# Eight dilated heads computed in two softmax parts and joined by their denominators, with the second block's weight units split inside both projections

## The chip, the cores and the metric

The kernel runs on one core of one Trainium2 chip. The metric is the device time in microseconds (us) of one execution, the median of a few runs. The core's engines work side by side and meet at semaphores: PE (TensorE: matrix products and transposes into PSUM), DVE (VectorE), ACT (ScalarE), POOL (GpSimd) and SP, which here does nothing but start transfers. ACT and POOL start transfers as well.

## The reference, cut to what matters

Two transformer blocks over 1024 tokens of width 1024. The first block's attention has 16 heads of width 64, eight dilated and eight of a 16 x 64 grid neighbourhood. A dilated head mixes three patterns:

```python
DIL_PATTERNS = ((128, 1), (512, 4), (2048, 16))
def dilated_mixture_attention(q, k, v, slopes):
    results = [dilated_window_attention(q, k, v, slopes, w, d) for (w, d) in DIL_PATTERNS]
    outs, lses = jnp.stack([r[0] for r in results]), jnp.stack([r[1] for r in results])
    weights = jax.nn.softmax(lses, axis=0)
    return jnp.sum(weights[..., None] * outs, axis=0).astype(q.dtype)
```

A query t sees the keys within 64 tokens, the keys within 256 tokens at a distance that 4 divides, and all keys at a distance that 16 divides, each with a bias of slope times distance. The mixture weighted by the log-sum-exps is one softmax in which a key counts as often as patterns hold it. So the keys of a query are a near band (|d| <= 64) and a far part of the same residue mod 4 (256 of 1024 keys). After attention come an RMS norm of each half of the heads, W_out, a router and 16 experts, and then the second block, whose first projection uses w_in2.

## The kernel before, in words

Every float32 product is made of three: a weight or activation x is split into hi (x rounded by a cast) and lo (x - hi), and hi*hi, hi*lo and lo*hi are summed. POOL splits weights: `split(n)` is a CAST (L661) and a TENSOR_TENSOR (L665) of 128x1024, one pair for each "unit" of weights, and PE has about 10.9 us of products for a unit.

**QKV projection.** 24 units of w_in (16 for Q and K, 8 for V). ACT takes a unit's result out of PSUM (L1412) in the order m = 0..23. Beside it DVE prepares tables for the second block's S5 scan: small operations first (helpers at L1795, L1800), then the first norm's spread root (L1746), which PE must have after unit 6, then eight sets of "turns" (L1929 to L1938). ACT sends a set off (L1418) in between its evacuations: for 6 <= m < 14 it waits for `turns_ready` and then issues the transfer, so a later evacuation stands behind it. PSUM has four slots, so PE can be a few units ahead of ACT.

**Attention.** One loop on each engine over steps t, 128 units: head u // 8, query tile u % 8. For unit u PE makes `scores` (L982: a 128-query tile against all 1024 keys for heads 0 to 7, against 256 or 384 keys for heads 8 to 15), DVE adds the bias and takes the row's maximum (L1984), ACT exponentiates with the sum (L1424), PE transposes (`turn`, L991), ACT copies (L1433), PE multiplies with the values (`mix`, L1005), DVE scales by the reciprocal (L1993, L1995). PE does scores(t), turn(t-2), mix(t-3) in a step. For each head POOL makes the split queries and keys QS, KH, KL, each half of the partitions (L697 to L703: three casts, three subtractions of 64x1024), starts the load of the head's bias strip, and then does `split_in2(h)` (L674, L676): one unit of w_in2. SP stores the two results to DRAM (w2_parts), waits, loads the next raw unit, and fills x_slots (the expert blocks' rows) with zeroes, 31 transfers of 512 KB in pieces of 512 bytes.

**End of attention.** Squares (L1440), a root, eight scalings of the dilated half at step T_SCALE (ACT copies turned blocks at L1453, the "f" copies) and of the other half at the end (DVE L2005), turned by `turn_na` (L1016) inside the first W_out units. SP gets to the loads of w_out (L633) after the last w_in2 unit is stored. The first two W_out units run together (`first_pair`, L865): k = 0..3 are the dilated half, k = 4..7 need the other half, with their lo parts (DVE L2010).

Of the kernel before, what the change touches and what calls it, by code (L numbers as in the profile page):

```python
# [18 lines left out]
STRIP = 1920  # L19
# [8 lines left out]
KSPLIT = 6  # L28
FF = 22
# [29 lines left out]
def key_tiles(h, i):  # L59

    if h < 8:
        return 0, 8
    return max(i - 1, 0), min(i + 2, 8)


def build(nc, xT, params, w_in, w_out, w_moe, w_in2, w_out2, w_up, w_down, dil_strip, na_strip, s5_b, s5_c, out):
# [5 lines left out]
    w2_parts = nc.dram_tensor("w2_parts", (18, 2, P, S), f32, kind="Internal").ap()  # L72
    s5_turns = nc.dram_tensor("s5_turns", (8, P, 2, S), f32, kind="Internal").ap()

    ctx = ExitStack()
    with ctx:
# [32 lines left out]
        negm = sb("negm", [P, 4])  # L109
        den = sb("den", [P, 8])  # L110
# [18 lines left out]
        def by_rows(ap):  # L129

            return ap.rearrange("p (c r) -> p r c", r=NA_ROWS)

        def by_columns(ap):

            return ap.rearrange("p (r c) -> p c r", c=NA_COLS)

        def columns(ap):

            return ap.rearrange("p (c r) -> p c r", r=NA_ROWS)

        def mat(name, c=0, n=P):
# [10 lines left out]
        x_again = sem("x_again")  # L152
# [4 lines left out]
        zero_set, slots_zeroed, x_scattered = sem("zero_set"), sem("slots_zeroed"), sem("x_scattered")  # L157
# [7 lines left out]
        member_ready, rank_read, dispatch_ready, xtm_ready = (  # L165
            sem("member_ready"), sem("rank_read"), sem("dispatch_ready"), sem("xtm_ready"))
# [4 lines left out]
        gains_ready, tsq_ready, tsum_taken, tvar_ready, troot_ready, tdiag_ready, hn_ready, hres_ready = (  # L171
            sem("gains_ready"), sem("tsq_ready"), sem("tsum_taken"), sem("tvar_ready"), sem("troot_ready"),
# [3 lines left out]
            sem("sq_ready"), sem("sq_added"), sem("sums_ready"), sem("std_ready"))  # L176
        parked, vt2_ready, low_split = sem("parked"), sem("vt2_ready"), sem("low_split")
# [7 lines left out]
        up_scaled, slots_ready = sem("up_scaled"), sem("slots_ready")  # L185
        qk_scaled, cst_again = sem("qk_scaled"), sem("cst_again")
# [5 lines left out]
        gdiff_ready, gexp_done, tdiff_ready, texp_done = (  # L192
            sem("gdiff_ready"), sem("gexp_done"), sem("tdiff_ready"), sem("texp_done"))
# [4 lines left out]
        conv_ready, gates_ready, tanh_ready, root_ready, ggate_ready, rg_ready = (  # L198
            sem("conv_ready"), sem("gates_ready"), sem("tanh_ready"), sem("root_ready"), sem("ggate_ready"), sem("rg_ready"))
        s5b_ready, s5bT_ready, s5x_ready, s5y_ready, s5g_ready, s5s_ready, s5_ready = (  # L200
            sem("s5b_ready"), sem("s5bT_ready"), sem("s5x_ready"), sem("s5y_ready"), sem("s5g_ready"), sem("s5s_ready"), sem("s5_ready"))
# [5 lines left out]
        conv0_ready, conv1_ready, gelu_ready, ffact_ready = (  # L207
            sem("conv0_ready"), sem("conv1_ready"), sem("gelu_ready"), sem("ffact_ready"))
# [17 lines left out]
        parts_order = list(range(0, U_OUT)) + list(range(U_IN2, U_OUT2)) + list(range(U_OUT, U_IN2)) + list(range(U_OUT2, len(units)))  # L226
# [13 lines left out]
        loads, raw_loads = {}, {}  # L240
        into = [0] * RING
        for u in parts_order:
            at_ring = 0 if in2(u) else ring_at(u)
            into[at_ring] += 16
            (raw_loads if in2(u) else loads)[u] = into[at_ring]
# [306 lines left out]
        troots = small[:, 6:8, :]  # L552


        @block.sync
        def _(sp):
            def experts():

# [2088 lines left out]
```

## Time and profile before

| | |
|---|---|
| time, median of 3 runs | 2444.22 us (2443.25 to 2449.57) |
| the profiled execution's own time, span | 2445.05 us, 2443.2 us |
| mean granted clock of PE | 0.964 |
| PE busy | 2263.9 us (93%) |
| PE weight load, DVE, POOL, ACT busy | 1774.0, 1165.3, 985.5, 578.2 us |

The span is what the profiler saw of one execution; its own time is the device time of the same execution. Busy times of engines overlap and don't add. With PE busy for 93% of the span, the kernel's time is nearly the time of PE's work where PE has work, and the question is where it hasn't.

### The profile page before, as it was taken

Reading aid. Unit: us, or ns where it says so; the run is one execution under the profiler, and the core shown is the slowest. Engines: PE = TensorE matmul, PEld = TensorE weight load, DVE = VectorE, ACT = ScalarE, POOL = GpSimd, SP = SyncE. Lnnn points to the kernel's source line nnn. Section 1 sums busy time; section 2 is a strip of 40 time slices with the busy share of each in tenths; the row PEclk is TensorE's granted clock in tenths of the full one; section 3 lists DMA queues with packets and bytes.
Section 4 is the critical chain, followed back from the end, with each engine's and each line's share of the span. In section 5 each row is a group of like instructions: output and inputs, shape, how many; then the busy total and the mean of one; then the engine's idle time right before and its main releaser. Section 6 shows DMA issues by size and latency. Waiting matters only on the chain.

```text
span 2443.2 us, 28063 instructions
## 1 busy us (share of the span) xinstructions
PE 2263.9 (93%) x10832; PEld 1774.0 (73%) x10832; DVE 1165.3 (48%) x1895; ACT 578.2 (24%) x831; POOL 985.5 (40%) x600
## 2 busy tenths in 40 slices
PE   7999999997699499999599998899999999999997
PEld 5888799987576366665376556678788888888875
DVE  7996644446413222222588777755432233143145
ACT  3101255566533111111231005221210011011011
POOL 2333554468623765700303862233323333333324
PEclk9999999998899699999799999899999999999998
DMA  4231154335622787822722221211111111111103
GB/s 156 78 121 70 42 188 144 120 110 170 201 99 113 271 301 299 324 104 97 280 76 86 103 74 47 104 38 49 43 46 50 52 48 39 61 50 39 58 26 112
DMA packets 89392, 274.33 MB, mean 112 GB/s; under 512 B 6896, under 2 KB 38768, under 8 KB 82096
## 3 DMA queue, kind: packets, MB, share of 16 engines
q1 hardware_dynamic: 71120, 188.84, 22.1%
q0 software_dynamic: 8064, 42.80, 4.8%
q10 hardware_dynamic: 10080, 40.90, 4.3%
q8 instruction: 90, 1.47, 0.2%
q14 instruction: 38, 0.31, 0.0%
HBM read 195.97 MB, written 76.55 MB: 112 GB/s over the span
## 4 chain that ended last, share of the span: by engine, by line
PE 79%; DVE 8%; POOL 5%; DMA 4%; issue 3%; ACT 2%; SPq 0%; DVEq 0%; POOLq 0%; ACTq 0%
PE ps L883 15%; PE ps L885 15%; PE ps L887 15%; PE ps L1005 5%; PE ps L1102 4%; PE ps L982 3%; PE ps L991 3%; PE ps L1086 2%; PE ps L1082 2%; PE ps L1084 2%; PE ps L1083 2%; PE ps L865 1%; PE ps L868 1%; PE ps L867 1%; PE ps L1070 1%
## 5 line engine op out<-in xcount | busy, mean ns | idle before, releaser
L883 PE MATMUL ps<-work_part 128*128 128x512 f32 x1760 | 547.9, 393 | 2.6 <-DVE work L2385 1.7
L887 PE MATMUL ps<-work_part 128*128 128x512 f32 x1760 | 542.4, 389 | 0.0
L661 POOL CAST work_part<-ring 128x1024 fp32r<-128x1024 f32 (+2 forms) x124 | 118.5, 956 | 786.1 <-PE ps L887 659.6
L883 PEld LDWEIGHTS ps<-work_part 128*128 128x128 f32 x1760 | 329.8, 188 | 76.9 <-issue 6.5
L887 PEld LDWEIGHTS ps<-work_part 128*128 128x128 f32 x1760 | 330.6, 188 | 69.2
L885 PE MATMUL ps<-work_part 128*128 128x512 f32 x1152 | 354.6, 389 | 0.0
L665 POOL TENSOR_TENSOR work_part<-ring,work_part 128x1024 fp32r<-128x1024 f32 (+2 forms) x124 | 281.2, 2268 | 15.9 <-PE ps L1300 6.1
L885 PEld LDWEIGHTS ps<-work_part 128*128 128x128 f32 x1152 | 216.2, 188 | 44.9
L885 PE MATMUL ps<-hT_part,work_part 128*128 128x512 f32 x608 | 188.0, 390 | 0.0
L1005 PE MATMUL ps<-work,hT 128*128 128x64 f32 x1376 | 174.3, 276 | 2.6 <-ACT hT L1433 2.1
L2033 DVE TENSOR_TENSOR hT<-ps,hT 128x1024 f32<-128x1024 f32 x40 | 49.0, 1225 | 261.5 <-PE ps L887 245.0
L1005 PEld LDWEIGHTS ps<-work,hT 128*128 128x128 f32 x1376 | 167.5, 195 | 6.8 <-ACT hT L1433 3.8
L885 PEld LDWEIGHTS ps<-hT_part,work_part 128*128 128x128 f32 x608 | 114.4, 188 | 24.1
L1984 DVE CUSTOM_DVE_ANT_0 hT<-ps,hT 128x1024 f32<-128x1024 f32 (+2 forms) x86 | 75.1, 874 | 116.0 <-PE ps L982 113.0
L982 PE MATMUL ps<-work_part 128*128 128x512 f32 (+2 forms) x384 | 115.3, 410 | 15.5 <-issue 7.9
L1701 ACT ACTIVATE work<-ps,cst 128x1024 f32<-128x1024 f32 x22 | 26.6, 1208 | 398.2 <-DVE ps L2455 398.2
L739 POOL TENSOR_TENSOR experts_lo<-pages,experts_hi 128x1024 fp32r<-128x1024 f32 x48 | 113.5, 2365 | 11.1 <-DMA pages<-w_moe 7.7
L1102 PE MATMUL ps<-pages,work 128*128 x248 | 111.6, 592 | 1.6 <-DVE work L2165 1.6
L865 PE MATMUL ps<-work_part 128*128 128x512 f32 x160 | 66.3, 414 | 48.3 <-POOL work_part L665 18.8
L1424 ACT ACTIVATE hT<-hT,negm 128x1024 f32<-128x1024 f32 (+2 forms) x86 | 74.6, 868 | 92.9 <-DVE negm L1984 92.7
L2455 DVE TENSOR_TENSOR ps<-ps,cst 128x1024 f32<-128x1024 f32 x22 | 27.1, 1232 | 144.2 <-PE ps L887 137.6
L1433 ACT ACTIVATE hT<-ps 128x1024 f32<-128x1024 f32 (+2 forms) x128 | 92.8, 725 | 0.8 <-PE ps L991 0.7
(376 smaller groups left out, 3490.2 us busy)
## 6 DMA issues: line engine op xcount, KB each, us to landing
pages<-w_moe SPq DMA_DIRECT2D x16, 2048.0 KB, 9.7
ring<-w_up_units SPq DMA_DIRECT2D x44, 512.0 KB, 3.2
ring<-w_in_units SPq DMA_DIRECT2D x42, 512.0 KB, 3.7
w_parts<-work_part SPq DMA_DIRECT2D x36, 512.0 KB, 3.6
work_part<-w_parts SPq DMA_DIRECT2D x36, 512.0 KB, 4.1
pages<-w_moe SPq DMA_DIRECT2D x16, 1024.0 KB, 7.0
x_slots<-hT SPq DMA_DIRECT2D x31, 512.0 KB, 5.2
work<-x_slots ACTq DMA_DIRECT2D x31, 512.0 KB, 5.7
```

The lines of the kernel that those rows point to most:

```text
L661: pool.tensor_copy(WHI[n % 2][:, 0:cols], w).then_inc(whi_ready, 1)
L665: pool.tensor_tensor(WLO[n % 2][:, 0:cols], w, WHI_F[n % 2][:, 0:cols], ALU.subtract).then_inc(wlo_ready, 1)
L739: lo = pool.tensor_tensor(XLOW[:, at_lo:at_lo + S], w, hi.bitcast(f32), ALU.subtract)
L865: mm = pe.matmul(pss[i][:, c], ws[i][0][:, w], hi[k][:, c], start=(k == 0), stop=(lo is None and k == last))
L883: pe.matmul(ps[:, c], whi[:, w], hi[k][:, c], start=(k == 0), stop=False)
L885: pe.matmul(ps[:, c], whi[:, w], lo[k][:, c], start=False, stop=False)
L887: mm = pe.matmul(ps[:, c], wlo[:, w], hi[k][:, c], start=False, stop=(k == len(hi) - 1))
L982: mm = pe.matmul(ps[:, b * HALF:b * HALF + w], QS[h % 2][:, i * P:(i + 1) * P], part[h % 2][:, c0:c0 + w], start=(part is KH), stop=(part ...
L1005: mm = pe.matmul(ps[:, 0:DH], PT[u % 2][:, j * P:(j + 1) * P], Wp[16 + k0 + j][:, h * DH:(h + 1) * DH], start=(j == 0), stop=(j == k1 - k0 ...
L1102: mm = pe.matmul(ps[:, half * HALF:(half + 1) * HALF], HAT[b % 2][:, f * P:(f + 1) * P], xw[:, bass.ds(pages[b] + 4 * S + f * S + half * H ...
L1433: act.activation(PT[u % 2][:, 0:(k1 - k0) * P], PS[bank(n)][:, 0:(k1 - k0) * P], ACT.Copy).then_inc(pT_ready, 1)
L1984: dve.tensor_tensor_reduce(out=banks(SB[u % 3][:, 0:nk]), in0=scores, in1=banks(bias), scale=-1.0, scalar=3.0e38, op0=ALU.add, op1=ALU.min ...
```

## The change

A dilated head becomes four units instead of eight (`NU` = 64 instead of 128). Units q = 0, 1 are the far part: four groups of 128 queries of one residue mod 4, each against that residue's 256 keys; units q = 2, 3 are the near band: four query tiles each against 256 keys around the tile. Each unit has four segments of 256 columns, with a maximum and a sum of its own. K and V of the dilated heads are stored by residue. The far part's output, maximum and sum (66 numbers a query) go through DRAM (`turn_rows`) to come back in token order, and `merge_diffs` (DVE), `merge_exps` (ACT), `merge_weights` (DVE) and `merge` (POOL) join them with the near part. Neighbourhood heads get four units of two tiles each. The other halves of KH and KL are copied by transfers (`double`, SP) instead of two POOL operations. The w_in2 units are split by POOL after units 1 to 12 of the QKV projection (`EARLY`) and after units 26 to 31 in W_out (`LATE`), from buffers of their own; the zeroing of x_slots moves to ACT's queue during V's units. The steps `T_SQ, T_ROOT, T_SCALE, T_TURN, T_PART` move with the shorter loop. Several semaphores are merged with no other effect on the order.

```diff
-STRIP = 1920
+STRIP = 896
+EARLY, LATE = 12, 6
+NR, NA_ = 4, 256
+HEAD_ROW = DH + 2
...
-        NU = NH * NT
-        T_SQ, T_ROOT, T_SCALE, T_TURN, T_PART = 72, 82, 84, 86, 97
+        T_DIFF, T_EXP, T_WEIGHT = 10, 11, 12
+        T_SQ, T_ROOT, T_SCALE, T_TURN, T_PART = 44, 48, 49, 51, 60
...
+            def double(h):
+
+                own, other = halves_of(h)
+                sp.wait_ge(qk_parts, 4 * (h + 1))
+                for part in (KH, KL):
+                    sp.dma_start(part[h % 2][other, :].bitcast(f32), part[h % 2][own, :].bitcast(f32)).then_inc(dup_loaded[h % 2], 16)
+
+            def turn_rows(h):
+
+                sp.wait_ge(heads_done, 4 * h + 2)
+                sp.dma_start(head_rows[h % 2].rearrange("(u p r) e -> p r u e", u=2, r=NR), OB[h % 2].rearrange("p (r u) e -> p r u e", u=2)).then_inc(rows_stored, 16)
+                sp.wait_ge(rows_stored, 16 * (h + 1))
+                if h >= 2:
+                    sp.wait_ge(merged, h - 1)
+                sp.dma_start(OBN[h % 2], head_rows[h % 2].rearrange("(t p) e -> p t e", p=P)).then_inc(rows_loaded[h % 2], 16)
...
-                    sp.wait_ge(zero_set, 1)
-                    for n in range(U_OUT2 - U_IN2):
-                        park_in2(n)
-                        for b in range(2 * n, min(2 * n + 2, NBLK)):
-                            if b >= 4:
-                                sp.wait_ge(scores_ready, NU // (NBLK + 1) * (b - 3))
...
+                    double(0)
+                    load_near_values()
+                    double(1)
+                    for h in range(2, NH):
+                        if h < 10:
+                            turn_rows(h - 2)
+                        double(h)
...
+            def merge(h):
+
+                far, rows = OBN[h % 2][:, :, 0:DH], bT[:, :, h * DH:(h + 1) * DH]
+                w = [stats(h, 2 + n).unsqueeze(2).to_broadcast([P, NT, DH]) for n in range(2)]
+                pool.wait_ge(weights_ready, h + 1)
+                pool.wait_ge(heads_done, 4 * h + 4)
+                pool.tensor_tensor(far, far, w[1], ALU.mult)
+                link(pool.tensor_tensor(rows, rows, w[0], ALU.mult))
+                pool.tensor_tensor(rows, rows, far, ALU.add).then_inc(merged, 1)
+                pool.wait_ge(merged, h + 1)
 
             for n in range(24):
                 split(n)
+                if 1 <= n <= EARLY:
+                    split_in2(n - 1)
...
-                pool.tensor_tensor(KL[h % 2][other, :], k[own, :], KH[h % 2][own, :].bitcast(f32), ALU.subtract).then_inc(qk_parts, 1)
-                pool.tensor_copy(KH[h % 2][other, :], k[own, :]).then_inc(qk_parts, 1)
...
-                pool.wait_ge(qk_parts, 6 * h + 6)
-                split_in2(h)
...
+                if 3 <= h < 11:
+                    merge(h - 3)
...
             for n in range(26, 32):
                 split(n)
+                split_in2(EARLY + n - 26)
...
+                if t % 4 == T_DIFF % 4 and 0 <= t - T_DIFF < DIL_UNITS:
+                    merge_diffs((t - T_DIFF) // 4)
+                if t % 4 == T_WEIGHT % 4 and 0 <= t - T_WEIGHT < DIL_UNITS:
+                    merge_weights((t - T_WEIGHT) // 4)
```

POOL in the QKV projection of the changed kernel, from the split of unit 4 on (part_loaded is the arrival of a raw w_in2 unit):

```order
L773 CAST work_part<-ring 128x1024 [waits mm_done,w_loaded0,wlo_ready]
L777 TENSOR_TENSOR work_part<-ring,work_part 128x1024 [waits whi_ready]
L783 CAST work_part<-work 128x1024 [waits part_loaded1]
L785 TENSOR_TENSOR work_part<-work,work_part 128x1024 [waits whi_ready]
L773 CAST work_part<-ring 128x1024 [waits mm_done,w_loaded1,wlo_ready]
```

Before, the rows at L773 and L777 (there L661 and L665) followed one another with nothing between; now a pair of w_in2 stands between every two of units 1 to 13.

POOL in attention, one dilated head of the kernel before:

```order
L697 CAST work_part<-work 64x1024 [waits qk_parts,wlo_ready]
L698 CAST work_part<-work 64x1024
L700 TENSOR_TENSOR work_part<-work,work_part 64x1024 [waits qk_parts]
L701 TENSOR_TENSOR work_part<-work,work_part 64x1024
L702 TENSOR_TENSOR work_part<-work,work_part 64x1024
L703 CAST work_part<-work 64x1024
L712 DMA hT<-dil_strip 128x1920
L674 CAST work_part<-ring 128x1024 [waits parked,w_loaded0,qk_parts]
L676 TENSOR_TENSOR work_part<-ring,work_part 128x1024 [waits whi_ready]
```

and of the changed one (head 0's merge, then head 4's splits and strip):

```order
L801 TENSOR_TENSOR hT<-hT 128x8x64 [waits heads_done,weights_ready]
L802 TENSOR_TENSOR work<-work,hT 128x8x64
L803 TENSOR_TENSOR work<-work,hT 128x8x64 [waits pool_link]
L826 CAST work_part<-work 64x1024 [waits qk_parts,mm_done,qk_scaled,merged]
L827 CAST work_part<-work 64x1024
L829 TENSOR_TENSOR work_part<-work,work_part 64x1024 [waits qk_parts]
L830 TENSOR_TENSOR work_part<-work,work_part 64x1024
L835 DMA hT<-dil_strip 128x896 [waits scores_ready]
```

The merge of head h-3, which waits for DVE's weights, now stands ahead of the splits of head h+1.

SP in attention of the changed kernel (the copies of head 3's keys, the row transfers of head 2, the copies of head 4's keys):

```order
L669 DMA work_part<-work_part 64x1024 [waits qk_parts]
L669 DMA work_part<-work_part 64x1024
L674 DMA head_rows<-hT 512x2x66 [waits heads_done]
L678 DMA hT<-head_rows 128x8x66 [waits merged,rows_stored]
L669 DMA work_part<-work_part 64x1024 [waits qk_parts]
L669 DMA work_part<-work_part 64x1024
```

Where stores of w_in2 units and zeroes stood, the copies for a head's keys now stand behind the row transfers of the head two earlier, and behind the wait for the first of them to land.

## Rows read from the trace of the kernel before

**Rows 1.** Windows: stretch, us, busy of each engine, PEclk, DMA share, GB/s.

```profile
85.30:205.30 120.00, 120.00 (x528) 98.67 (x527) 113.82 (x338) 14.79 (x10) 39.07 (x22) 1.00 0.30 110
294.30:522.00 227.70, 224.96 (x1739) 209.88 (x1740) 103.33 (x253) 137.22 (x192) 120.73 (x78) 1.00 0.43 143
522.00:651.10 129.10, 112.52 (x743) 100.07 (x742) 74.76 (x273) 83.86 (x228) 101.00 (x63) 0.92 0.53 172
```

**Rows 2.** Timeline, DVE and POOL around one split: start, duration, engine, line.

```profile
75.08 0.17 DVE L1795 TENSOR_SCALAR small<-small 128x2 f32<-128x2 f32 x1
...
75.29 1.06 POOL L661 CAST work_part<-ring 128x1024 fp32r<-128x1024 f32 x1 [7.35 <-PE ps L887]
75.48 0.90 DVE L1795 TENSOR_SCALAR small<-small 128x2 f32<-128x2 f32 x1
...
76.44 2.41 POOL L665 TENSOR_TENSOR work_part<-ring,work_part 128x1024 fp32r<-128x1024 f32 x1
76.61 2.26 DVE L1795 TENSOR_SCALAR small<-small 128x2 f32<-128x2 f32 x1
```

**Rows 3.** Timeline, DVE and ACT in the QKV projection.

```profile
85.53 1.23 DVE L1746 TENSOR_TENSOR work<-std,cst 128x1024 f32<-128x1024 f32 x1
...
96.95 1.97 ACT L1412 ACTIVATE work<-ps 128x1024 f32<-128x1024 f32 x1 [8.89 <-PE ps L887]
...
205.67 0.33 ACTq L1418 DMA_DIRECT2D s_turns<-work  x1
...
219.36 1.03 ACT L1412 ACTIVATE work<-ps 128x1024 f32<-128x1024 f32 x1 [9.58 <-PE ps L968]
```

**Rows 4.** Timeline, one step of a dilated head.

```profile
380.29 1.19 PE L982 MATMUL ps<-work_part 128*128 128x512 f32 x4
...
381.52 1.23 DVE L1984 CUSTOM_DVE_ANT_0 hT<-ps,hT 128x1024 f32<-128x1024 f32 x1 [1.88 <-PE ps L982]
...
383.90 0.48 PE L982 MATMUL ps<-work_part 128*128 128x512 f32 x1
```

**Rows 5.** Timeline, POOL's parts of a head.

```profile
590.34 2.36 POOL L700 TENSOR_TENSOR work_part<-work,work_part 64x1024 fp32r<-64x1024 f32 x1
```

**Rows 6.** Groups by line, busy, mean ns: a copy of 1024 columns.

```profile
L2172 DVE COPY work<-ps 128x1024 f32<-128x1024 f32 x5 | 6.1, 1224 | 12.8 <-PE ps L1102 12.8
```

**Rows 7.** DMA issues: KB each, median us from issue to landing.

```profile
x_slots<-hT SPq DMA_DIRECT2D x31, 512.0 KB, 5.2
...
outT<-hT SPq DMA_DIRECT2D x16, 256.0 KB, 2.2
```

**Rows 8.** Timeline, steps of a neighbourhood head.

```profile
635.78 0.42 DVE L1984 CUSTOM_DVE_ANT_0 hT<-ps,hT 128x256 f32<-128x256 f32 x1 [1.36 <-DMA hT<-na_strip]
...
636.25 0.51 ACT L1424 ACTIVATE hT<-hT,negm 128x256 f32<-128x256 f32 x1 [1.21 <-DVE negm L1984]
...
638.33 0.62 PE L982 MATMUL ps<-work_part 128*128 128x384 f32 x2
...
640.00 0.45 PE L982 MATMUL ps<-work_part 128*128 128x384 f32 x1 [0.34 <-DVE work L1995]
```

**Rows 9.** Timeline, steps in which dilated tiles are turned and copied.

```profile
576.02 0.59 PE L982 MATMUL ps<-work_part 128*128 128x384 f32 x2 [1.15 <-issue]
...
578.91 0.59 PE L982 MATMUL ps<-work_part 128*128 128x384 f32 x2 [1.15 <-issue]
```

**Rows 10.** Timeline, from the end of attention into W_out.

```profile
658.51 3.25 DVE L2005 TENSOR_SCALAR work<-work,small 128x512 f32<-128x512 f32 x8
...
662.30 11.12 SPq L633 DMA_DIRECT2D ring<-w_out_units  x6
...
669.89 0.77 PE L865 MATMUL ps<-work_part 128*128 128x512 f32 x1 [18.79 <-POOL work_part L665]
...
681.97 1.92 PE L1016 MATMUL ps<-cst,work 128*128 128x128 f32 x16
...
689.39 0.50 PE L865 MATMUL ps<-work_part 128*128 128x512 f32 x1 [2.77 <-DVE work_part L2010]
```

More of the change, by code:

```diff
@@ L225, in build @@
         split_of = {u: n for n, u in enumerate(split_units)}
-        parts_order = list(range(0, U_OUT)) + list(range(U_IN2, U_OUT2)) + list(range(U_OUT, U_IN2)) + list(range(U_OUT2, len(units)))
+        parts_order = []
+        for u in range(0, U_IN2):
+            parts_order.append(u)
+            if 1 <= u <= EARLY:
+                parts_order.append(U_IN2 + u - 1)
+            if u >= U_IN2 - LATE:
+                parts_order.append(U_IN2 + EARLY + u - (U_IN2 - LATE))
+        parts_order += list(range(U_OUT2, len(units)))
         order_of = {u: n for n, u in enumerate(parts_order)}
@@ L238, in wparts @@
             return WHI[split_of[u] % 2], WLO[split_of[u] % 2]
-        loads, raw_loads = {}, {}
+        loads = {}
         into = [0] * RING
         for u in parts_order:
-            at_ring = 0 if in2(u) else ring_at(u)
-            into[at_ring] += 16
-            (raw_loads if in2(u) else loads)[u] = into[at_ring]
+            if in2(u):
+                continue
+            into[ring_at(u)] += 16
+            loads[u] = into[ring_at(u)]
             if u == U_IN2 - 1:
@@ L315, in build @@
         U_QKV += [take(1) for m in range(2, 7)]
-        n_mix = add_late_norm(Hp, "norm_mix", [Wp[22], Wp[23], Wp[15]], mix_use, take(1), (BHI, [hTr[t][:, :] for t in range(NT)]))
+        n_mix = add_late_norm(Hp, "norm_mix", [Wp[22], Wp[23], Wp[11]], mix_use, take(1), (BHI, [hTr[t][:, :] for t in range(NT)]))
         U_QKV += [take(1) for m in range(7, 16)]
@@ L633, in _ @@
                     sp.dma_start(ring[:, ring_at(u), 0:src.shape[-1]], src).then_inc(w_loaded[ring_at(u)], 16)
+                if u == 4:
+                    load_in2(0)
+                    load_in2(1)
+                if 5 <= u < EARLY + 5:
+                    park_in2(u - 5)
+                if u == U_OUT + 5:
+                    sp.wait_ge(mm_done, done(use_o[NU - 1]))
+                    load_in2(EARLY)
+                    load_in2(EARLY + 1)
+                if u == U_IN2 - 1:
+                    for n in range(EARLY, EARLY + LATE):
+                        park_in2(n)
             for half in range(2):
@@ L711, in _ @@
[L711 to L719 removed]
+                    pool.wait_ge(scores_ready, PARTS_DONE[4 * (h - 1)])
@@ L1397, in _ @@
             for m in range(24):
-                if m >= 16:
-                    if m == 16:
-                        for i in range(4):
-                            act.wait_ge(turns_stored[i], 32)
+                if m == 16:
+                    for i in range(4):
+                        act.wait_ge(turns_stored[i], 32)
+                    link(act.activation(ZERO, ident, ACT.Copy, scale=0.0))
+                if m == 23:
+                    act.wait_ge(slots_zeroed, 16 * NBLK)
+                if m in (12, 14):
+                    act.wait_ge(parked, 32 * (EARLY - 1 + (m - 12) // 2))
                 n = U_QKV[m] if m < 16 else U_V[m - 16]
@@ L1432, in copy_pT @@
                     act.wait_ge(mm_done, done(use_o[u - 2]))
-                act.activation(PT[u % 2][:, 0:(k1 - k0) * P], PS[bank(n)][:, 0:(k1 - k0) * P], ACT.Copy).then_inc(pT_ready, 1)
+                act.activation(PT[u % 2][:, cols], PS[bank(n)][:, cols], ACT.Copy).then_inc(pT_ready, 1)
             def heads_square(half, i):
-                act.wait_ge(heads_done, (7 + 8 * half) * NT + i + 1)
+                if half == 0:
+                    act.wait_ge(merged, 8)
+                else:
+                    act.wait_ge(heads_done, NU - 4 + i // 2 + 1)
                 if half + i:
```

460 lines of the change are left out of this document (283 added, 177 removed).

## The prediction

> **What bounds the kernel now.** I read the windows by stage first. In the QKV projection PE is busy for all of 120.00 us of the stretch 85.3 to 205.3, but DVE has 113.82 of the same 120: one engine is the bound and another has nearly no room. In the dilated heads' stretch PE is busy for 224.96 of 227.70, in the neighbourhood heads' for 112.52 of 129.10 [rows 1]. So PE's work sets the dilated heads, and links between engines take 16.6 us from the neighbourhood heads. Then the timeline from the end of attention: the stretch ends at 651.1, W_out starts at 669.89 after a wait for POOL's split, which had waited for a load that SP issued only at 662.30 [rows 10].
>
> **The change, part by part.**
>
> *QKV projection, +32.* POOL's pair for one unit is a CAST of 1.06 and a TENSOR_TENSOR of 2.41, with 120.00 us for 528 products, 48 to a unit, or 10.9 us a unit of PE's work over it [rows 1, 2]; twelve more pairs fit in POOL's time. They don't fit in DVE's. A DVE operation that takes 0.17 us took 0.90 beside the CAST and 2.26 beside the TENSOR_TENSOR: DVE stood until POOL's instruction was over, 0.73 + 2.09 = 2.8 us for one split [rows 2]. This is what a port held by one of the two looks like. The Trainium skill, "SBUF — State Buffer", § Who interferes with whom, has the rule for it (the shared port pair is an exclusive lock, the engine that comes first keeps it for its instruction); the trace agrees at 0.90 and 2.26, and by the rule the delay is a whole instruction for each split, as the rows have it. Twelve added splits cost DVE 12 x 2.8 = 34, and the longer DVE works the more ordinary splits it meets, one each 10.9 us: 3 to 4 more in the 34 us, of which I take 2, 5.6 (the late sets need not meet each). That is 40. DVE's last set of turns, sent off at 205.67, comes at about 245.7. What slack is there? ACT takes the first V unit transposed at 219.36, 9.6 us after it was free for it, and DVE was ready before [rows 3]. The same 10 us lie at the front: the norm's root is done at 85.53 + 1.23 = 86.8 and unit 6, which it must follow, at 96.95 [rows 3]. So 40 - 10 = 30 reach PE. I expect about 17 of it at the norm's root after unit 6, and 13 at the evacuations behind `turns_ready`. A PE that has stood so long restarts at the lower clock (after the idle before 669.89 a product took 0.77, the one at 689.39 took 0.50 [rows 10]): 2 more.
>
> *Dilated heads.* Before, a step takes 383.90 - 380.29 = 3.6 us of PE [rows 4], eight to a head. A unit after is as many PE columns: scores of 8 products of 256 against 4 of 512, the same 8 turns, 8 groups of two in place of a chain of eight in the mix. So a unit costs PE 3.65 and a head 14.6 instead of 29: the work halves because half the units are gone. But a new chain goes round through the engines. The scores of head h+1 wait for `double(h+1)`, that waits for POOL's splits of h+1, and those stand behind merge(h-3) in POOL's order. The merge waits for DVE's `merge_weights(h-3)`, which DVE does in step 4h, behind the bias and maximum of head h's first scores. So a head's splits can't begin before the head ahead of it has begun. Its length, from rows: from the first scores on, DVE's bias of 1024 columns 1.23 [rows 4], now in four pieces, 1.5; the evacuating copy of 256 columns a quarter of 1.22 [rows 6] plus its fixed part, 0.4; five small operations with a link each at 0.2, 1.0; PE's scores before it 1.2 [rows 4]; sum 4.1. POOL's three merges of 512 columns, half of 2.36 each [rows 5], plus three links, 3.8; sum 7.9. The splits, two casts of 1.05 and two subtractions of 2.36, 6.9; sum 14.8. The pair of 256-KB copies: issue 0.33 twice [rows 3] and a landing of 2.2 by the 256-KB row [rows 7], or 2.9; sum 17.7 to 18.4. I take 18.2 a head, against PE's 14.6. Nothing in it runs beside anything else of it. Heads 3 to 7: 5 x 18.2 = 91. Head 0 needs nothing of POOL in attention but its own splits: 10.4 from the stretch's start, which lies a unit into it. Heads 1 and 2 have no merge ahead, but their copies behind the row transfers: 16 each, 32.
>
> ACT has four exponentials of 256 columns at 0.51 [rows 8] and a copy of 1.03 (the 1024 columns at 219.36 [rows 3]) in a unit, 3.05 of 3.65: not the bound.
>
> *Neighbourhood heads.* POOL still does the merges of heads 5 to 7 ahead of the splits of heads 9 to 11 (3 x 17.3 = 52 for heads 8 to 10; the first scores are shorter). The last 20 steps: a tile took 640.00 - 638.33 = 1.67 with 0.34 of it idle [rows 8], so two tiles in a unit are 2.7 of PE and one link where two were, 2.75. Twelve steps less one, 11 x 2.75 = 30.3. In the eight steps with f copies ACT's queue puts copy_f between copy_pT and the next exponentials: before a step took 578.91 - 576.02 = 2.9 [rows 9], and with two tiles' worth in ACT it is 2.9 + 0.9 (a wider exponential and copy) + 0.4 (a second bias) = 4.2: 33.6. Squares and table loads 3, the tail of three steps without scores 6. Together 72.9.
>
> Attention after: 10.4 + 32 + 91 + 52 + 72.9 = 258.3, before 227.7 + 129.1 = 356.8 [rows 1]: -98.5.
>
> *W_out's start, -15.2.* Call the end of attention E (651.1, where the last window of [rows 1] ends). Before, k = 4 of the first pair starts at 689.39, E + 38.3 [rows 10]. Now the w_in2 stores are not ahead of the w_out loads on SP, and POOL's split(24) runs as soon as the last scores are done, so PE's k = 0..3 start before the other half's scales. Those end for four tiles at 658.51 + 4 x 0.4 = E + 9 [rows 10]; the first turns stand there, four groups of six products, 6 x 120.00/528 = 1.36 each [rows 1], lie between, and the second turns start at E + 15.7. From there to k = 4 it was 689.39 - 681.97 = 7.4 [rows 10], so E + 23.1.
>
> *At nothing.* The LATE pairs in W_out: POOL has two pairs of 3.5 [rows 2] a unit against 10.9 of PE; their cover gone, 6 x 3.5 = 21 at the most, and DVE's work there is little. The zeroing, 31 transfers that were on SP beside attention, is now 31 x 512 KB beside V's units; its price is hidden unless SP's weight loads come late (a range term, 0 to 8). DVE's merge weights, the smaller strips and merged semaphores lie in other engines' gaps.
>
> Sum: 2445.05 + 32 - 98.5 - 15.2 = 2363.4; the profiled execution was 0.8 over the median, so 2362.
>
> **The rivals.**
>
> *(a) The round through POOL is hidden* (the chain is shorter than 14.6, or queued early enough). Then heads 1 to 7 cost 14.6 and heads 8 to 10 about 11, a gain of 7 x 3 + 3 x 6.5 = 40: 2322. For it: POOL was busy for only 120.73 of 227.70 [rows 1]. Against: the order of its rows, merge ahead of splits.
>
> *(b) DVE's delay doesn't reach PE* (the added splits fall where DVE has its PSUM or one-operand work). 2362 - 32 = 2330. Against: 113.82 busy of 120 [rows 1], whatever the operation.
>
> *(c) The row transfers are slow.* The far rows are 1024 pieces of 264 bytes out and in, and `double(h+2)` stands behind the landing of head h's store. The store starts in step 4h+5 and head h+2 needs its keys in step 4h+8, so a second way round is the store's time S, the copies' 2.9, a step of 3.65 and a link or two: S + 7.5. It is longer than 18.2 from S = 10.7 on. The nearest row, 1024 pieces of 512 bytes, has 5.2 with neighbours in flight [rows 7]: hidden. If S is 15 to 18, eight heads (2 to 9) take 22.5 to 25.5 in place of 18.2: 34 to 58 more, 2396 to 2420. The Trainium skill, "DMA: Bandwidth & Descriptors", § Specifications, speaks for it: below 512 bytes the engines read, modify and write. No row here shows a smaller piece; by it the store might take twice the zeroing's time, 10.4, an estimate, which is still hidden.
>
> *(d) Slower than before.* Only (c) carried further does it. My sum has 82 us to lose over eight heads, 10.2 each: a period of 28.4, an S of 21, four times the zeroing's 5.2 [rows 7]. At S = 23 the time is 2461.
>
> **How the numbers follow.** My own course 0.64, (a) 0.12, (b) 0.10, (c) 0.10, (d) 0.02, and 0.02 for what none of them holds. The bounds of unknown prices: the delay of QKV from 0 to 45, the chain 14.6 to 20 a head (-40 to +16), the W_out start from -10 to -20, the hidden parts up to +8. The range 2314 to 2408 holds my course, (a), (b) and the near half of (c). Within 0.3% (7 us, about what a measurement tells from no change) is hardly a case: it needs (c) with S just at 21. Faster (my course, (a), (b), (c)) 0.96, same 0.01, slower 0.03, with half of the unnamed rest.
>
> **What would show it.** In the changed kernel's trace: PE idle for some 17 us after unit 6, with DVE's L1746 row late at about 114 against 85.5; the first V evacuation near 250 against 219. In attention, heads' first scores released by the copies of keys (L669), 18 us apart, and POOL's cast released by `merged`. At W_out, k = 4 at 23 us after the last mix. The prediction is wrong if POOL's splits are ready a head ahead, if DVE's small operations don't stand beside the new pairs, or if a row store lasts over 10.

## The result, and the profile after

The changed kernel takes 2421.68 us (median of 4 runs, 2419.63 to 2423.71) against 2445.59 for the kernel before on the same chip: a ratio of 0.9901, interval 0.9883 to 0.9918. That is 24 us less. I had forecast 2362, 82 less, with a range of 2314 to 2408: the direction is right, the size is wrong by more than the range allows. Later runs of the kernel before, beside the experiments, had medians of 2442.6, 2442.8 and 2442.0, so a difference of medians between an experiment and the changed kernel comes out up to 4 us larger than by the ratios.

Where did it go? I read the times at which the stages meet. First ACT's row in the V units and PE's in attention:

```profile
247.45 1.03 ACT L1567 ACTIVATE work<-ps 128x1024 f32<-128x1024 f32 x1
...
316.25 1.03 ACT L1567 ACTIVATE work<-ps 128x1024 f32<-128x1024 f32 x1 [10.78 <-PE ps L1082]
329.42 1.02 ACT L1567 ACTIVATE work<-ps 128x1024 f32<-128x1024 f32 x1 [12.14 <-DMA x_slots<-work]
```

The first V unit is taken at 247.45, where 219.36 stood [rows 3] and I had expected about 250. The last but one is taken at 316.25; in the kernel before the same row stands at 290.10. The last one should follow 3 us later, as it did before (293.20), and comes at 329.42: what ended its wait is the landing of the zeroes. PE's first scores start at 330.49 instead of 294.3.

The windows of the changed kernel from there (columns as in [rows 1]), head by head for heads 0 to 10, then the last heads, and W_out up to k = 4:

```profile
330.50:342.50 12.00, 10.51 (x68) 10.30 (x69) 5.81 (x32) 10.38 (x35) 4.24 (x3) 0.78 0.41 98
342.50:362.10 19.60, 17.34 (x135) 17.23 (x134) 7.21 (x36) 12.60 (x37) 7.59 (x7) 0.93 0.32 79
362.10:381.80 19.70, 17.76 (x132) 17.62 (x133) 7.54 (x39) 12.04 (x37) 2.63 (x2) 0.91 0.32 79
381.80:405.30 23.50, 18.16 (x133) 18.08 (x133) 9.98 (x44) 12.04 (x37) 10.50 (x8) 0.88 0.29 66
405.30:428.20 22.90, 18.31 (x132) 18.17 (x133) 9.86 (x44) 12.04 (x37) 10.51 (x8) 0.87 0.28 67
428.20:452.40 24.20, 24.17 (x132) 24.20 (x133) 8.24 (x44) 10.88 (x35) 10.45 (x8) 0.60 0.28 64
452.40:474.30 21.90, 16.93 (x135) 16.83 (x134) 10.85 (x44) 13.20 (x41) 10.54 (x8) 0.94 0.29 70
474.30:498.30 24.00, 17.99 (x133) 17.88 (x133) 10.13 (x44) 12.04 (x37) 10.51 (x8) 0.86 0.32 65
498.30:519.70 21.40, 14.09 (x102) 13.81 (x102) 8.97 (x28) 8.27 (x21) 10.51 (x8) 0.82 0.33 72
519.70:541.20 21.50, 11.66 (x82) 11.29 (x82) 8.53 (x32) 7.68 (x21) 10.47 (x8) 0.74 0.21 47
541.20:562.20 21.00, 14.39 (x82) 13.99 (x82) 6.08 (x29) 7.57 (x20) 16.69 (x12) 0.74 0.20 48
562.20:640.00 77.80, 66.51 (x487) 63.80 (x487) 42.96 (x140) 56.27 (x138) 30.40 (x21) 0.92 0.31 85
640.00:664.40 24.40, 17.45 (x81) 14.57 (x80) 5.08 (x12) 15.85 (x21) 1.52 (x2) 0.86 0.58 237
```

Heads 3 to 7 take 22 to 24 us each, not 18.2, and in four of the five PE is busy for 17 to 18 of it. The head from 428.2 on shows a second thing: PE is busy for all of 24.17 us, with the same work, at a granted clock of 0.60. Attention as a whole lasts 640.0 - 330.5 = 309.5 us against 356.8 before. From its end to k = 4 of the first pair it is 24.4, where it was 38.3 [rows 10].

| stretch | forecast | measured |
|---|---|---|
| start of attention | +32 | +36.2 (26.2 at the V unit before the last, 10.0 more at the last) |
| attention | -98.5 | -47.3 |
| its end to k = 4 | -15.2 | -13.9 |
| the rest | 0 | -0.4 |

Sum -25.4, which is what the spans differ by (2443.2 and 2417.8). So nothing behind W_out moves, and one term is wrong by 51.

What does a head wait for? The waits of PE in attention (us in total, times, longest), and the timeline of one round, on PE, POOL and SP:

```profile
PE ps L1095 <- DMA work_part<-work_part: 48.9, 9, 9.9
```

```profile
405.26 2.22 PE L1095 MATMUL ps<-work_part 128*128 128x256 f32 x8 [5.31 <-DMA work_part<-work_part]
...
410.42 1.03 POOL L801 TENSOR_TENSOR hT<-hT 128x512 f32<-128x512 f32 x1 [12.64 <-DVE hT L2184]
...
412.54 1.19 POOL L803 TENSOR_TENSOR work<-work,hT 128x512 f32<-128x512 f32 x1
413.79 1.04 POOL L826 CAST work_part<-work 64x1024 fp32r<-64x1024 f32 x1
...
418.33 2.37 POOL L830 TENSOR_TENSOR work_part<-work,work_part 64x1024 fp32r<-64x1024 f32 x1
...
420.73 1.10 SPq L669 DMA_DIRECT2D work_part<-work_part  x2
...
428.23 2.23 PE L1095 MATMUL ps<-work_part 128*128 128x256 f32 x8 [4.62 <-DMA work_part<-work_part]
```

The round is the one of the forecast, link for link: from the first scores to the merge 5.2 us (forecast 4.1), merge 3.4 (3.8), splits 6.9 (6.9), and from the issue of the two key copies to the scores that wait for them 7.5 (2.9 to 3.6). The copies and row transfers in the table of DMA issues (KB each, median us to landing):

```profile
work_part<-work_part SPq DMA_DIRECT2D x32, 256.0 KB, 6.0
head_rows<-hT SPq DMA_DIRECT2D x8, 264.0 KB, 4.9
hT<-head_rows SPq DMA_DIRECT2D x8, 264.0 KB, 3.1
```

A key copy, 64 partitions of SBUF to 64 others, lands after 6.0 us, where I had taken 2.2 from a transfer of the same size, but from 128 partitions to DRAM [rows 7]. The row transfers in pieces of 264 bytes, which I had feared, land in 4.9 and 3.1.

### The profile page after: what moved, and what is told of

Read it like the earlier page. It is cut to its first block, busy times and chain, and to the rows that moved or that the text cites. A ratio compares the mean times of both kernels' runs of the same rounds, so it can differ in the third digit from the quotient of the medians.

```text
span 2417.8 us, 26338 instructions
## 1 busy us (share of the span) xinstructions
PE 2177.0 (90%) x10096; PEld 1707.9 (71%) x10096; DVE 1163.9 (48%) x1927; ACT 524.3 (22%) x904; POOL 955.9 (40%) x591
## 4 chain that ended last, share of the span: by engine, by line
PE 65%; DVE 17%; DMA 5%; POOL 5%; issue 4%; ACT 4%; SPq 0%; DVEq 0%; POOLq 0%; ACTq 0%
PE ps L997 13%; PE ps L999 13%; PE ps L1001 13%; PE ps L1251 4%; PE ps L1235 2%; PE ps L1231 2%; DMA work_part<-work_part 2%; PE ps L1233 2%; PE ps L1095 2%; PE ps L1232 2%; DVE work L2104 1%; DVE work L2106 1%; PE ps L1155 1%; DVE small L1970 1%; DVE work L2108 1%
## 5 line engine op out<-in xcount | busy, mean ns | idle before, releaser
L773 POOL CAST work_part<-ring 128x1024 fp32r<-128x1024 f32 (+2 forms) x124 | 118.9, 959 | 761.4 <-PE ps L1001 631.3
L997 PEld LDWEIGHTS ps<-work_part 128*128 128x128 f32 x1760 | 330.2, 188 | 79.3 <-issue 6.9
L1001 PEld LDWEIGHTS ps<-work_part 128*128 128x128 f32 x1760 | 330.7, 188 | 69.1
L777 POOL TENSOR_TENSOR work_part<-ring,work_part 128x1024 fp32r<-128x1024 f32 (+2 forms) x124 | 282.3, 2277 | 15.9 <-PE ps L1449 6.1
L999 PEld LDWEIGHTS ps<-work_part 128*128 128x128 f32 x1152 | 216.2, 188 | 44.9
L1095 PE MATMUL ps<-work_part 128*128 128x256 f32 (+2 forms) x416 | 90.2, 364 | 67.6 <-DMA work_part<-work_part 48.9
L999 PEld LDWEIGHTS ps<-hT_part,work_part 128*128 128x128 f32 x608 | 114.7, 189 | 24.2
L1095 PEld LDWEIGHTS ps<-work_part 128*128 128x128 f32 x416 | 75.1, 246 | 70.0 <-issue 58.3
L1155 PE MATMUL ps<-work,hT 128*128 128x64 f32 x864 | 113.8, 288 | 5.2 <-ACT hT L1597 5.2
L1155 PEld LDWEIGHTS ps<-work,hT 128*128 128x128 f32 x864 | 112.6, 209 | 6.4 <-ACT hT L1597 3.6
L2149 DVE CUSTOM_DVE_ANT_0 hT<-ps,hT 128x256 f32<-128x256 f32 (+1 forms) x130 | 52.4, 453 | 118.6 <-PE ps L1095 105.5
L1251 PEld LDWEIGHTS ps<-pages,work 128*128 128x128 f32 x248 | 47.1, 190 | 60.7 <-issue 60.7
```

The lines of the kernel that those rows point to most:

```text
L773: pool.tensor_copy(WHI[n % 2][:, 0:cols], w).then_inc(whi_ready, 1)
L777: pool.tensor_tensor(WLO[n % 2][:, 0:cols], w, WHI_F[n % 2][:, 0:cols], ALU.subtract).then_inc(wlo_ready, 1)
L997: pe.matmul(ps[:, c], whi[:, w], hi[k][:, c], start=(k == 0), stop=False)
L999: pe.matmul(ps[:, c], whi[:, w], lo[k][:, c], start=False, stop=False)
L1001: mm = pe.matmul(ps[:, c], wlo[:, w], hi[k][:, c], start=False, stop=(k == len(hi) - 1))
L1095: mm = pe.matmul(o, lhs, of_part(part), start=(part is keys[0]), stop=(part is keys[1]))
```

## The experiments

**Splits ahead of the merge.** Is the round what costs, or is PE slow by itself? Two orders are exchanged at once, on POOL (splits and merge) and on SP (key copies and row transfers).

```diff
-                if 3 <= h < 11:
-                    merge(h - 3)
+                if 4 <= h < 12:
+                    pool.wait_ge(qk_parts, 4 * h + 4)
+                    merge(h - 4)
...
+                        double(h)
                         if h < 10:
                             turn_rows(h - 2)
-                        double(h)
```

> POOL does the splits of head h before the merge of head h-4 (the merges one head later), and SP starts the key copies of a head ahead of the row transfers. Nothing is left out. Theory (the round of weights, merge, splits and key copies sets a head's time in attention: 21.0 to 24.2 us a head for heads 3 to 10): the splits and copies are ready before PE needs them, a dilated head takes about 15.5 and heads 8 to 10 about 11, so 5 x 7.8 + 3 x 10.3 + some 8 for heads 1 and 2 = about 78 us less than the changed kernel, near 2344. First rival (PE itself is slow in the new units, at the lower clock, whatever it waits for): a head stays above 20 and the time above 2400. Second rival (the row transfers set the head's time): no change either, since they are as before.

2356.18 us (2353.5 to 2361.01), ratio 0.9643, interval 0.9627 to 0.9659: 65 less than the changed kernel, of the 78 expected. In its waits of PE over attention the key copies have all but gone:

```profile
PE ps L1096 <- ACT work L1568: 11.2, 1, 11.2
...
PE ps L1096 <- DMA work_part<-work_part: 1.0, 1, 1.0
```

The window of one dilated head, and its four scores on PE's timeline:

```profile
381.88:398.59 16.71, 16.71 (x134) 16.71 (x134) 8.65 (x44) 12.06 (x39) 10.49 (x9) 1.00 0.46 92
```

```profile
381.88 2.12 PE L1096 MATMUL ps<-work_part 128*128 128x256 f32 x8
...
386.42 2.12 PE L1096 MATMUL ps<-work_part 128*128 128x256 f32 x8
...
390.96 1.41 PE L1096 MATMUL ps<-work_part 128*128 128x128 f32 x10
...
394.79 1.36 PE L1096 MATMUL ps<-work_part 128*128 128x256 f32 x10
```

The head is now all PE, at the full clock. It also shows a second mis-sizing: a far unit takes 4.54 us and a near one 3.83, so a head is 16.7 of PE, not 14.6. Which of the two exchanges gave how much wasn't tried apart. In the changed kernel's round above, SP issues the copies at 420.73, as POOL's last split ends (418.33 + 2.37): for heads 3 to 10 POOL's order counted, and SP's can have counted only for the first heads, whose copies stood behind a row store of 4.7 and 5.0 us.

The whole of attention, from the first scores to W_out's first product, in the changed kernel and in this one:

```profile
330.49:640.53 310.04, 247.86 (x1744) 243.23 (x1745) 136.46 (x557) 175.57 (x494) 135.58 (x98) 0.85 0.30 72
332.00:578.53 246.53, 231.63 (x1744) 228.00 (x1745) 130.64 (x557) 175.40 (x494) 135.74 (x98) 0.94 0.38 90
```

Of the 63.5 us less, 48 are PE's waits for the copies (48.9 down to 1.0). Nearly all the rest, 16.2, is PE's busy time: the same 1744 products at a granted clock of 0.94 instead of 0.85.

**POOL makes the second halves.** Undoes `double` alone (two transfers of 256 KB less, a subtraction and a cast of POOL more in each head).

```diff
-                pe.wait_ge(qk_parts, 4 * (h + 1))
-                pe.wait_ge(dup_loaded[h % 2], 32 * (h // 2 + 1))
+                pe.wait_ge(qk_parts, 6 * (h + 1))
...
+                pool.tensor_tensor(KL[h % 2][other, :], k[own, :], KH[h % 2][own, :].bitcast(f32), ALU.subtract).then_inc(qk_parts, 1)
+                pool.tensor_copy(KH[h % 2][other, :], k[own, :]).then_inc(qk_parts, 1)
```

> Undoes one part of the change: POOL makes the second halves of KL and KH itself (a subtraction and a cast of 64x1024, 3.4 us a head) and the two transfers of 256 KB are gone. Nothing is left out. Theory (the copies' 7.5 us from issue to the first scores is on the path): the round goes from 23.0 to about 19, some 4 less for each of heads 3 to 10 and 3 for heads 1 and 2: about 2385. Rival (the copies are not what is waited for; POOL is): POOL's 3.4 more for each of eight heads comes on top, about 2449.

2398.27 us (2394.22 to 2399.46), ratio 0.9816, interval 0.98 to 0.9833: 21 to 23 less, where 36 was expected and the rival said 27 more. The expected round was 19 us. One is 19.8 (the first merge rows of two heads stand at 404.79 and 424.61), but the seven from 383.70 to 528.05 have a mean of 20.6, against 22.6 in the changed kernel (386.99 to 545.00). One of them is set by PE at the lower clock and not by the round:

```profile
440.50:465.00 24.50, 24.50 (x136) 24.50 (x136) 8.74 (x44) 13.13 (x41) 13.76 (x10) 0.65 0.18 48
```

So the copies were on the path and cost more than the 3.4 us of POOL that they replaced, but by 2 us a round, where I had expected 4.

**Half of each key copy.** From head 2 on a copy moves 512 of 1024 columns.

```diff
+                w = slice(0, S if h < 2 else HALF)
                 for part in (KH, KL):
-                    sp.dma_start(part[h % 2][other, :].bitcast(f32), part[h % 2][own, :].bitcast(f32)).then_inc(dup_loaded[h % 2], 16)
+                    sp.dma_start(part[h % 2][other, w].bitcast(f32), part[h % 2][own, w].bitcast(f32)).then_inc(dup_loaded[h % 2], 16)
```

> On the changed kernel. From head 2 on each key copy moves 512 of the 1024 columns (the rest of the other half keeps older data, so the output is not the reference's); same number of transfers and rows, half the bytes. Theory (the copies' time goes by their bytes, 64 partitions to 64 partitions): a landing of 3.5 to 4 instead of 6, and 2 to 2.5 us less on each of heads 2 to 10, so about 20 less, 2402. Rival (a fixed time to land, or waiting behind other transfers): landing still near 6 and 2417 to 2424.

2401.51 us (2399.93 to 2403.23), ratio 0.9826, interval 0.9805 to 0.9848: the 20 expected. But the landing went only from 6.0 us to 4.7 (median of the 28 halved copies), and PE's wait for the copies from 48.9 to 32.3. Half the bytes took off a fifth of the time: the time expected came, the price by bytes alone did not. What the fixed part is, stays open.

**The early w_in2 splits, narrowed.** Ten of the twelve units have 8 of 1024 columns split.

```diff
+                w = slice(0, 8 if 2 <= n < EARLY else S)
-                pool.tensor_copy(RAW_HI[at], RAW[at]).then_inc(whi_ready, 1)
+                pool.tensor_copy(RAW_HI[at][:, w], RAW[at][:, w]).then_inc(whi_ready, 1)
```

(the subtraction in the same way, and the store of lo takes the tile of hi).

> Leaves out work: ten of the twelve w_in2 units that POOL splits in the QKV projection get only 8 of their 1024 columns split (the stores and loads of these units stay), so the output is not the reference's. Theory (DVE stands while POOL's instruction runs, and that delay reaches PE): DVE's last set of turns is ready some 28 us earlier and the first V unit is taken about 22 to 26 us earlier; 2396 to 2400 in all. Rival (DVE and ACT are late for another reason, the stores and raw loads or the order on ACT's queue): within 5 us of the changed kernel, 2417 to 2424.

2395.02 us (2389.78 to 2396.01), ratio 0.9807, interval 0.9791 to 0.9823: 23 to 27 less. The two last V units are taken at 291.06 and 304.91, 25.2 and 24.5 earlier than in the changed kernel. All transfers were still there, and only ten of POOL's twelve added pairs had become short, so it is these instructions that make DVE late, and with it PE.

**The zeroing divided.** Sixteen blocks in the V units, fifteen copied DRAM to DRAM in attention.

```diff
-                    act.wait_ge(slots_zeroed, 16 * NBLK)
+                    act.wait_ge(slots_zeroed, 16 * ZF)
...
+                        for b in ((ZF, ZF + 1) if h == 2 else (ZF + h - 1,)):
+                            sp.dma_start(x_slots[b * P:(b + 1) * P, :], x_slots[(b - ZF) * P:(b - ZF + 1) * P, :]).then_inc(slots_zeroed, 16)
```

> Of the 31 zeroing transfers 16 stay in the V units on ACT's queue, four a unit; the other 15 blocks are copied from zeroed ones, DRAM to DRAM, by SP in attention, one or two a head. Nothing is left out. Theory (the last V unit's evacuation waits 10 us for the zeroes to land): the last V unit is taken at about 320 instead of 329.4, and the time is about 10 less, 2411. Rival (something else is late there, the values' rows or the first keys' copies, or the copies in attention hold up the key copies): 0 to 10 more, 2421 to 2431.

2413.57 us (2410.62 to 2422.03), ratio 0.9878, interval 0.9861 to 0.9894, which overlaps the changed kernel's: by time alone it is not clear. The trace is:

```profile
319.41 1.03 ACT L1572 ACTIVATE work<-ps 128x1024 f32<-128x1024 f32 x1 [10.76 <-PE ps L1087]
322.59 1.02 ACT L1572 ACTIVATE work<-ps 128x1024 f32<-128x1024 f32 x1 [2.16 <-PE ps L1087]
```

The last V unit follows the one before it by 3.2 us again, released by PE. It is taken 6.8 earlier than 329.42. The one before it is 3.2 later than in the changed kernel; I have no cause for this, but it is at 316.2 to 318.4 in the four other kernels that leave the projection as it is. The profiled execution is the slowest of the four (2422.03; the others 2410.62 to 2413.64), so only this stretch is read from it.

**Both edits.** Splits first, and the zeroing divided.

> Splits ahead of the merge and the zeroing divided, in one kernel, nothing left out. If the two gains are apart in the program (the attention loop, 65 us; the last V unit's wait, 8 us), they add: about 2348. If the fifteen DRAM copies now disturb an attention loop that has become tight (the key copies and row transfers share the queues with them), part is lost: 2352 to 2360.

2348.7 us (2346.05 to 2352.96), ratio 0.9614, interval 0.9591 to 0.9637: 73 less than the changed kernel, where the two alone had 65 and 8: they add, as far as can be told when the runs of one kernel lie 7 us apart.

**Far queries side by side.** On the kernel with the splits first.

```diff
-                        lhs = queries.rearrange("p (u x r) -> p r u x", u=2, r=NR)[:, r, n % 2, :]
+                        lhs = queries[:, n * P:(n + 1) * P]
```

> On the kernel with the splits first. The far units read their queries as 128 neighbouring columns instead of every fourth one, so the scores are of the wrong queries and the output is not the reference's; all counts and sizes are the same. Theory (PE's load of a weight tile with a stride takes 0.24 us instead of 0.12, which shows as 2.12 us for the 8 products of a far unit against 1.36 for 10 of a near one): about 0.75 less for each of 16 far units, 12 in all, 2344. Rival (the far scores are slow for another reason, the keys' columns or the PSUM banks): no change, 2356.

2344.91 us (2336.9 to 2347.7), ratio 0.9582, interval 0.9554 to 0.9609, against 0.9643: 11 to 15 less. In attention's groups of instructions (by form) the scores of 256 columns, first with every fourth column, then with plain queries:

```profile
L1096 PE MATMUL ps<-work_part 128*128 128x256 f32 x256 | 56.7, 359 | 14.6 <-ACT work L1568 11.2 <-issue 2.4 <-DMA work_part<-work_part 1.0
L1096 PE MATMUL ps<-work_part 128*128 128x256 f32 x256 | 43.8, 307 | 15.3 <-ACT work L1568 11.8 <-issue 2.3 <-DMA work_part<-work_part 1.1
```

The 256 products, half of them in far units, take 43.8 us instead of 56.7. The scores of a head's two far units there:

```profile
392.65 1.20 PE L1096 MATMUL ps<-work_part 128*128 128x256 f32 x8
396.27 1.20 PE L1096 MATMUL ps<-work_part 128*128 128x256 f32 x8
```

A far unit is 3.62 us long here instead of 4.54. So the strided weight tile is what makes the far units 0.9 longer, at the full clock. At the lower of PE's two levels it shows much less: in the first heads, at a granted clock of 0.50, eight plain products took 2.05 us (345.96) and eight strided ones 2.21 in the kernel with the splits first (344.34).

**The w_in2 units in the heads.** On both edits, the twelve early units are split in attention again, behind the merge, one a head.

```diff
-                if 1 <= n <= EARLY:
-                    split_in2(n - 1)
...
+                if h in AT_HEAD:
+                    pool.wait_ge(qk_parts, 4 * h + 4)
+                    split_in2(AT_HEAD[h])
```

> On the kernel of both edits: the twelve w_in2 units that were split in the QKV projection are split in attention again, one a head in heads 0 to 7 and 12 to 15, behind the merge; SP stores and loads them there. Nothing is left out. Theory (twelve added pairs cost the projection about 26 us through DVE, and POOL has 5.6 us left of a dilated head's 16.7 with the splits first): the first V unit is back near 219 to 222 and the time about 26 less than the kernel of both edits, 2322. Rival (the attention loop has no room left: POOL's 3.5 more, and the stores' bytes beside the key copies, make PE wait again): the gain in the projection is given back in attention, 2335 to 2350.

2355.71 us (2351.21 to 2357.16), ratio 0.9631, interval 0.9608 to 0.9654: 7 more than without it by the medians, with intervals that overlap, and 34 more than expected. The projection gave back what was expected (the last V unit at 294.04), and attention took 279.6 us (295.1 to 574.7). As the rival said, the gain in the projection was lost in attention, and 6 us more than its 2350. But was it POOL's time? Its DMA issues:

```profile
ring<-w_in_units SPq DMA_DIRECT2D x36, 512.0 KB, 5.9
...
head_rows<-hT SPq DMA_DIRECT2D x8, 264.0 KB, 8.4
```

and POOL's timeline, with an idle time of 4 to 9.5 us ahead of each of the eleven splits from head 1 on, in six of them ended by the raw unit's landing:

```profile
353.77 1.03 POOL L804 CAST work_part<-ring 128x1024 fp32r<-128x1024 f32 x1 [8.49 <-DMA ring<-w_in_units]
```

The row stores land in 8.4 us, where they took 4.9 in the changed kernel and 5.5 in the one with both edits, and POOL stands where it should work. That speaks for the transfers, not POOL's 3.5 us; the next run tries it.

**The zeroes in the projection.** On the last kernel, all zeroing moved to where the DMA queues have room, and the next raw unit loaded as soon as the stores have landed.

```diff
-        ZERO = Wp[23][:, S - P:S]
+        ZERO = Wp[15][:, S - P:S]
...
+                for b in range(3 * (u - 5), min(3 * (u - 4), NBLK)) if u >= 5 else ():
+                    sp.dma_start(x_slots[b * P:(b + 1) * P, :].rearrange("p (k n) -> p k n", n=P),
+                                 ZERO.unsqueeze(1).to_broadcast([P, NT, P])).then_inc(slots_zeroed, 16)
```

> On the kernel with the w_in2 units in the heads. All 31 zeroing transfers now lie in the QKV projection (three after each weight load of units 5 to 15, on SP, from a zeroed part of a tile that K's last unit fills later), the DRAM copies in attention are gone, and the next raw w_in2 unit is loaded as soon as the stores have landed. Nothing is left out. Theory (in the kernel before this one the transfers in attention lay in each other's way: row stores landed in 8.4 us instead of 4.9 and POOL waited 4 to 9 us a head for raw units): row stores land in 5 to 6 again, most of the 34 us lost in attention come back, 2322 to 2335. Rival (POOL's 3.5 us a head itself is too much for the loop, whatever the transfers do): 2345 to 2356.

2328.02 us (2324.36 to 2332.28), ratio 0.9519, interval 0.9493 to 0.9545. This kernel beats both: 114 less than the kernel before, 94 less than the changed one. Its DMA issues and two of its rows:

```profile
ring<-w_in_units SPq DMA_DIRECT2D x36, 512.0 KB, 4.0
...
head_rows<-hT SPq DMA_DIRECT2D x8, 264.0 KB, 6.3
```

```profile
294.23 3.20 PE L1121 MATMUL ps<-work_part 128*128 128x256 f32 x12 [1.11 <-ACT work L1592]
...
552.34 0.47 PE L1005 MATMUL ps<-work_part 128*128 128x512 f32 x1 [0.50 <-DVE work L2184]
```

Attention starts at 294.2, where it started before the change, and W_out at 552.3: 258.1 us with the twelve splits in it, against 279.6 in the last kernel and 248.5 (321.5 to 570.0) in the kernel of both edits, which has none there. So of the 31 us that the splits cost attention at first, 21.5 lay with the transfers. Where are the other 9.6? Windows of 16.7 us, counted from the first scores, show it: the second and the fifth of this kernel, then the second of the kernel of both edits.

```profile
310.93:327.63 16.70, 15.39 (x70) 15.42 (x71) 3.61 (x18) 5.97 (x18) 12.74 (x10) 0.51 0.58 170
361.03:377.73 16.70, 16.70 (x135) 16.70 (x133) 8.67 (x45) 12.05 (x38) 13.91 (x11) 1.00 0.71 193
```

```profile
338.19:354.89 16.70, 16.70 (x120) 16.70 (x121) 6.45 (x34) 9.53 (x30) 0.94 (x1) 0.86 0.31 79
```

In this kernel PE waits 4.56 us for head 1's key copies (2.78 in the kernel of both edits), and then works at 0.51 of the clock through the second window: 70 products instead of 120. The first three windows have 256 products against 323, half a head's work. From the fourth to the eighth PE is busy throughout at 1.00 in both kernels, and a round stays at 16.7 us with the 3.5 us of POOL in it (first merge rows at 375.35 and 392.05). So in those heads POOL's time costs nothing, and most of the 9.6 is lost in the first two. Whether a transfer or POOL's order makes head 1's copies late there wasn't tried. Two things were moved at once here (the zeroes, and the order of the raw load); which of them gave more wasn't tried either.

## Why the prediction was wrong

**The QKV projection: right in mechanism, and nearly in size.** The norm's spread root was late: DVE did it at 114.41, forecast about 114, and PE waited 17.2 us after unit 6, where I had said about 17:

```profile
115.69 3.78 PE L1060 MATMUL ps<-work,cst 128*128 128x512 f32 x4 [17.16 <-DVE work L1916]
...
242.20 0.33 ACTq L1576 DMA_DIRECT2D s_turns<-work  x1
```

The last set of turns is sent off at 242.2, forecast 245.7, before 205.67 [rows 3]. 26 of my 32 us arrived, and the narrowed splits took 25 of them away again, so this cause is shown. What the Trainium skill says in "SBUF — State Buffer", § Who interferes with whom, of a port pair locked for a whole instruction, fits these traces: DVE operations of 0.17 us took 0.90 and 2.26 beside POOL's CAST and TENSOR_TENSOR [rows 2].

**The wait for the zeroes: a step priced at nothing that cost 10.** I had called the zeroing "hidden unless SP's weight loads come late", and gave it 0 to 8. It did not delay a load; ACT itself waits for the zeroes before the last V unit, since they are read from a tile that this unit fills. In that stretch the DMA engines are busy throughout (share 1.01) and move 285 GB/s:

```profile
304.00:316.00 12.00, 12.00 (x60) 10.01 (x58) 9.75 (x3) 1.03 (x1) 8.49 (x5) 1.00 1.01 285
```

I had added up bytes, and had not read the wait as a deadline. With half of the zeroes elsewhere the wait was gone.

**Attention: the step that failed.** The prediction says "the pair of 256-KB copies: issue 0.33 twice and a landing of 2.2 by the 256-KB row, or 2.9", and from it 18.2 us a head, with 20 as the most that the range allowed. The round exists and closes as it says (splits first: 65 us gone), but the copies take 7.5 us from issue to use, and a round 23.0. The row that I took the 2.2 from carries the same bytes from 128 partitions to DRAM; these go from 64 partitions of SBUF to 64 others, and there are two at once. Half the bytes landed in 4.7, so bytes are a part of the price; whether the partitions, the way inside SBUF or the pair makes the rest wasn't tried. Of the 51 us, heads 3 to 7 have 116.5 - 91 = 25.5, heads 8 to 10 12, heads 1 and 2, whose copies stand behind the row stores, 7.3, head 0 1.6, and the last heads with the tail 4.9. In a head of 23.0 the copies are 4 too many and the way to the weights 1.1.

That 1.1 is the far unit's scores, 2.2 us where I had 1.2 from [rows 4]. Two things stand behind it, and neither alone would have mended it: they read strided weights, and they come right after PE's wait, at a granted clock of 0.52 (405.3 to 410.3), where eight plain products take 2.05 as well.

The clock is a third thing, and the forecast had it at nothing in attention. After a wait of 4.6 us the head from 428.2 ran near the lower of PE's two levels, 1.2 GHz (0.60 over the head), and PE took 24.2 us for it, longer than the round; the heads from 405.3 and 474.3, after waits as long, had 0.87 and 0.86. With the waits gone the window of a head has 1.00, and PE's busy time over attention is 16 us less. So a wait can be paid twice: once itself, once in slower work behind it.

**The rivals.** (a), the round hidden, didn't come, and its floor was also too low, 14.6 for a head that needs 16.7 of PE, mostly because the far units' weights are read with a stride (0.9 for each of two units). (b) is refuted by the 17.2 us wait and by the narrowed splits. (c), slow row transfers, is refuted: the store lands in 4.9, far from the 10.7 that it would need. I looked for the slow transfer in the small pieces and it was in the large ones beside them. (d) falls with (c).

**W_out's start.** 24.4 us against 23.1: right. Late splits and the rest of the program: at nothing, as said; the spans differ by the three stretches to 0.4 us.

## What to carry to other kernels

A transfer's price must come from a row with its own shape: the same memories, partitions and bytes; where none exists, the bound belongs into the range at its full length times the number of rounds. When a chain goes round through several engines, look at what stands ahead of what in one engine's order: exchanging two steps in POOL's queue and two in SP's gave 65 us with the same work on every engine. And work that is moved out of one stage goes where it has company: w_in2's splits cost 26 us beside DVE's small operations and some 10 in attention, once the transfers there were out of each other's way; the zeroes cost 10 in V's units and nothing that shows beside the Q and K units.

## What the runs showed of the hardware

A key copy of 256 KB inside SBUF, 64 partitions of 4 KB to 64 others, landed in 6.0 us (median of 32), with half the bytes in 4.7 (median of 28). 264 KB in 1024 pieces of 264 bytes went to DRAM in 4.9 and came back in 3.1. PE loads a weight tile of every fourth column slower than one of neighbouring columns: at the full clock 8 scores products of 256 columns took 2.12 us, with plain columns 1.20; at a granted clock of 0.50 it was 2.21 and 2.05. The same 1744 products of attention kept PE busy for 247.9 us with waits between them (granted clock 0.85) and for 231.6 without (0.94). Row stores that landed in 4.9 us, and in 5.5 with DRAM copies of 512 KB beside them, took 8.4 when loads and stores of 512 KB came on top.
